# DeltaNet decay factors: from matrix products with triangles of ones to rows of a running-sum table, loaded per head

## The chip, the cores and the metric

One core of a Trainium2 chip runs the whole program. The metric is the device time of one execution in microseconds (us); lower is better. Five engines run their own instruction streams and wait for each other by semaphores: TensorE (PE in the rows; its weight loads are PEld), VectorE (DVE), ScalarE (ACT), GpSimd (POOL) and SyncE (SP). SP streams the weights; POOL and ACT issue the other DMA transfers, each on its own queue.

## The reference

A two-layer diffusion step: a neighbourhood-attention layer, then a gated DeltaNet layer, on 128 context tokens and 256 latent tokens. The change concerns the DeltaNet layer alone, for each of 32 value heads and two scan directions:

```python
gc = jnp.cumsum(g, axis=-1)
decay = jnp.exp(jnp.where(incl, gc[..., :, None] - gc[..., None, :], -jnp.inf))
kb = k * beta[..., None]
a_mat = (jnp.where(strict, jnp.einsum('bhnid,bhnjd->bhnij', kb, k) * decay, 0.0)
         + jnp.eye(DN_CHUNK, dtype=jnp.float32))
...
qk = jnp.einsum('bhnid,bhnjd->bhnij', q, k) * decay
...
    o_i = (jnp.einsum('bhcd,bhde->bhce', q_i * jnp.exp(g_i)[..., None], s)
           + jnp.einsum('bhij,bhje->bhie', qk_i, v_new))
```

`g` is a log decay per token and head, `gc` its running sum inside a chunk (of 128 tokens in the kernel: one context chunk, two latent ones), `decay` the matrix of exp(gc_i - gc_j), and exp(gc_i) scales the queries.

## The kernel before, in words

Weights arrive as 512 KB half tiles. ScalarE rounds each to a high part (`split_hi`, L403), VectorE subtracts to get the low part (`split_lo`, L412), and TensorE multiplies with three matmuls per 128x128 block (`multiply`, L445 to L447). Eight blocks make a half tile; in the plans one block, three matmuls of 384 columns, is one **part**.

The DeltaNet layer runs in phases, each engine through its own copy of the same plan. `ba` projects the gates and sums `g` with triangles of ones into tables for all heads. `dnP` projects the first key head (96 parts, no recurrence). `dn0` is a loop of 8 turns, `dn1` one of 7: each turn computes the recurrence of one key head (two value heads `v`, two directions `d`, so four units `u`) and between its steps projects the next key head. `dnE` is the last recurrence alone. Between `dn0` and `dn1` stand `ysplitA`, `fetchA`, `outA` (half of the output projection) and `keep1`. On entering a phase an engine waits at a barrier (`barrier`) until all other engines have done every counted step of the phases before. Inside the loops there are no barriers.

The order inside a turn is `DN_PLAN`: `merge` spreads the 96 parts among the steps of the chain by weights, a step of weight w standing after about 0.9 w further parts. The steps that matter here, in order: `norms` (sums of squares of q and k on TensorE, then logarithm and exponential on ScalarE, each with a table load), `decay` 0 to 2 and `broad` 1 and 2, `unit` (VectorE scales q and k), `gram` 0 to 2, `values`, then the triangular inversion from `left1` to `xf`, `recall`, `apply`, `state`, `out` (the last output products), `squares` and `out_norm`. After `out` come 4 parts, and 4 more in the next turn before `norms`.

A decay matrix of chunk c is made thus: POOL multiplies a triangle of ones by `g` of the next head into `g_mask` (`mask_steps`, L1487, which borrows the buffer `inv_c`), TensorE multiplies that by the other triangle into a bank of PSUM (L680; for `broad` by all ones, L686), ScalarE exponentiates the bank into `decay` (L988) or `q_dec` (L992). In `gram` VectorE reads the product of k with k and with q from PSUM (L1291), multiplies by `decay` and beta into `inv_c` (L1298), adds the directions (L1304) and the identity (L1307), and multiplies `decay` for the outputs (L1310); POOL then makes the first inversion buffer from `inv_c` (`right`, L1508), for which `left1` waits on TensorE (L784). GpSimd ends a turn with the gated outputs (`y`, L1532). TensorE's products go in turn to a ring of four banks; a product waits until the reader of the one four places before is done (`ring_free`).

```python
wait_steps(pool, turn, ("dve", "g_now"), *which)
lone()
for u in range(4):
    d, v = u // 2, u % 2
    i = nc.gpsimd.tensor_scalar(g_mask[c][:, u, :], K["le" if d == 0 else "ge"],
                                g_now[:, c, d, v:v + 1], 1.0, ALU.mult, ALU.mult)
```

Of the kernel before, what the change touches and what calls it, by code (L numbers as in the profile page):

```python
# [31 lines left out]
P = 128  # L32
# [113 lines left out]
def with_ada(halves):  # L146
    plan = []
    for k in halves:
# [13 lines left out]
_chain = [(5, ("norms",)), (2.5, ("decay", 0)), (2, ("decay", 1)), (1.5, ("broad", 1)), (0, ("unit",)), (2, ("decay", 2)),  # L162
          (1.5, ("broad", 2)), (1, ("gram", 0)), (2, ("gram", 1)), (2, ("gram", 2)), (1, ("values", 0)),
# [31 lines left out]
def dn_products():  # L195

    made = []
    for item in DN_CHAIN:
        what, arg = item[0], item[1] if len(item) > 1 else None
        if what == "decay":  # L200
            made.append((f"decay{arg}", "act"))
        elif what == "broad":
            made.append((f"broad{arg}", "act"))
        elif what == "norms":
# [24 lines left out]
def emit(nc, known, dram):  # L229
# [4 lines left out]
    with ExitStack() as ctx:  # L234
# [100 lines left out]
        for c in range(CHUNKS):  # L335
# [7 lines left out]
        decay = [region.take(f"decay{c}", [P, 4, P]) for c in range(CHUNKS)]  # L343
        q_dec = [None] + [region.take(f"q_dec{c}", [P, 4, P]) for c in (1, 2)]
# [4 lines left out]
        g_mask = [inv["c", c] for c in range(CHUNKS)]  # L349
# [6 lines left out]
                                 "halves_done", "evacuated", "small_in", "pairs_in", "x_in", "x_out", "bias_in", "k_out",  # L356
# [218 lines left out]
        def _(pe):  # L575
# [77 lines left out]
            def ba(pe, phase, turn):  # L653
# [10 lines left out]
                for n, masks in enumerate((("le", "ge"), ("gt", "lt"), ("ones", "ones"))):  # L664
# [5 lines left out]
                    done("pe", f"sums{n}", mm)  # L670

            def dn(pe, phase, turn):
                for item in DN_PLANS[phase]:
# [3 lines left out]
                    elif what == "decay":  # L677
                        wait_steps(pe, turn, ("pool", f"g_mask{arg}", True), ring_free(f"decay{arg}"))
                        for d, mask in enumerate(("gt", "lt")):
                            mm = nc.tensor.matmul(ring(f"decay{arg}")[:, 2 * d * P:(2 * d + 2) * P], K[mask],  # L680
                                                  g_mask[arg][:, 2 * d:2 * d + 2, :].rearrange("p v i -> p (v i)"),
                                                  start=True, stop=True)
                        done("pe", f"decay{arg}", mm)
                    elif what == "broad":
                        wait_steps(pe, turn, ring_free(f"broad{arg}"))
                        mm = nc.tensor.matmul(ring(f"broad{arg}")[:], K["ones"],  # L686
# [690 lines left out]
        def _(pool):  # L1377
# [257 lines left out]
```

## Time and profile before

| what | value |
|---|---|
| median of 3 runs | 2961.02 us (2958.56 to 2961.33) |
| the profiled execution's own time | 2958.55 us |
| its span | 2957.0 us |
| busy share of the span: PE, PEld, DVE, ACT, POOL | 89%, 85%, 64%, 40%, 24% |
| mean granted TensorE clock | 0.95 |
| share of the DMA queues: q1 (SP), q0 (POOL), q10 (ACT) | 24.5%, 8.6%, 2.6% |

A row of the timeline gives the start, the time that the group took, the engine, the line, the operation with the tensors it writes and reads, and in brackets how long the engine had been idle and what ended that. Matmuls are pipelined, so their own times overlap; what one costs is the distance from one start to the next. An fp32 matmul is recorded as two passes. Attention fills the first third of the span; `ba` begins about 1014 us into it, `dn0` at 1087, `outA` at 1877, `dn1` at 2026 and `dnE` at 2716.

### The profile page before, as it was taken

The numbers are of one execution on the slowest core, as the hardware profiler recorded it, in microseconds if no ns is written. First come the engines' busy times: TensorE is split into PE (matmuls) and PEld (weight loads), VectorE is DVE, ScalarE is ACT, GpSimd is POOL, SyncE is SP. The second block draws the span as 40 slices with busy tenths as digits, with TensorE's granted clock in tenths as the row PEclk, the third lists the DMA queues.
The fourth block names the chain that finished last, engine by engine and source line by source line (L and its number), as shares of the span: only waits on it lengthen the run. The fifth ranks groups of instructions, "written<-read, shape, count | busy, mean of one in ns | idle before, by whom it ended". The sixth has DMA issues, their size and how long they took to land. (4 is left out here: it accounts for less than half of the span.)

```text
span 2957.0 us, 51408 instructions
## 1 busy us (share of the span) xinstructions
PE 2625.2 (89%) x15405; PEld 2514.3 (85%) x15405; DVE 1906.8 (64%) x3821; ACT 1179.7 (40%) x2167; POOL 716.8 (24%) x1293
## 2 busy tenths in 40 slices
PE   2458999999989699999999999898999999998797
PEld 2458999999989598888988898897988899887697
DVE  2878888888853547666666667434676667665433
ACT  1024333333333533544444444323535453544322
POOL 2302222222211112332333233102234323332210
PEclk9999999999999799999999999998999999999699
DMA  8565666666643132212212121333222222211042
GB/s 236 190 218 205 234 228 232 222 233 233 228 167 125 67 133 72 75 64 71 75 68 71 65 76 66 125 127 117 73 75 68 66 73 71 75 64 57 25 150 92
DMA packets 115644, 363.06 MB, mean 123 GB/s; under 512 B 29072, under 2 KB 31248, under 8 KB 114640
## 3 DMA queue, kind: packets, MB, share of 16 engines
q1 hardware_dynamic: 69408, 252.74, 24.5%
q0 software_dynamic: 21280, 87.44, 8.6%
q10 hardware_dynamic: 24848, 21.82, 2.6%
q14 instruction: 86, 0.70, 0.1%
q8 instruction: 22, 0.36, 0.0%
HBM read 346.22 MB, written 15.73 MB: 122 GB/s over the span
## 5 line engine op out<-in xcount | busy, mean ns | idle before, releaser
L445 PE MATMUL bank<-h_hi,w_hi 128*128 128x384 f32 x2576 | 998.7, 388 | 47.8 <-DVE h_lo L1118 34.0
L447 PE MATMUL bank<-h_hi,w_lo 128*128 128x384 f32 x2576 | 884.9, 344 | 0.0
L446 PE MATMUL bank<-h_lo,w_hi 128*128 128x384 f32 x2576 | 882.4, 343 | 0.0
L412 DVE TENSOR_TENSOR w_lo<-raw,w_hi 128x512 fp32r<-128x512 f32 (+1 forms) x610 | 560.1, 925 | 306.4 <-ACT w_hi L403 254.1
L403 ACT ACTIVATE w_hi<-raw 128x512 fp32r<-128x512 f32 (+1 forms) x610 | 461.6, 792 | 369.1 <-PE bank L447 336.5
L445 PEld LDWEIGHTS bank<-h_hi,w_hi 128*128 128x128 f32 x2576 | 501.5, 195 | 71.3 <-issue 45.7
L446 PEld LDWEIGHTS bank<-h_lo,w_hi 128*128 128x128 f32 x2576 | 503.0, 195 | 13.5 <-issue 7.2
L447 PEld LDWEIGHTS bank<-h_hi,w_lo 128*128 128x128 f32 x2576 | 497.5, 193 | 0.0
L1083 DVE SCALAR_TENSOR_TENSOR ada_terms<-raw_ada,cond_rows 128x1024 f32<-128x1024 f32 x256 | 312.7, 1222 | 11.2 <-DMA raw_ada<-in_late 6.7
L445 PE MATMUL bank<-y_hi,w_hi 128*128 128x384 f32 x768 | 264.1, 344 | 33.2 <-DVE y_lo L1188 22.3
L1525 POOL CAST inv_x<-inv_x 128x128 fp32r<-128x128 f32 x576 | 211.6, 402 | 258.9 <-DVE inv_x L1355 258.3
L446 PE MATMUL bank<-y_lo,w_hi 128*128 128x384 f32 x768 | 262.9, 342 | 0.0
L447 PE MATMUL bank<-y_hi,w_lo 128*128 128x384 f32 x768 | 262.7, 342 | 0.0
L960 ACT ACTIVATE inv_turn<-bank 128x256 fp32r<-128x256 f32 x288 | 109.2, 386 | 344.4 <-PE bank L784 343.8
L784 PE MATMUL bank<-consts,inv_x 128*128 128x128 f32 x576 | 120.6, 297 | 92.5 <-POOL inv_x L1508 80.7
L1349 DVE TENSOR_TENSOR inv_cross<-bank,pairs 128x256 fp32r<-128x256 f32 x288 | 115.4, 422 | 134.3 <-PE bank L788 133.8
L784 PEld LDWEIGHTS bank<-consts,inv_x 128*128 128x128 f32 x576 | 79.1, 148 | 119.9 <-POOL inv_x L1508 99.3
L588 PE MATMUL bank<-cond,raw 128*128 128x2 f32 x384 | 84.8, 353 | 108.0 <-DMA raw<-in_stream 56.5
L445 PEld LDWEIGHTS bank<-y_hi,w_hi 128*128 128x128 f32 x768 | 148.5, 193 | 35.4 <-issue 23.5
L1423 POOL DMA_DIRECT2D raw_ada<-in_late x128 | 68.8, 538 | 450.0 <-DVE ada_terms L1083 359.1
L588 PEld LDWEIGHTS bank<-cond,raw 128*128 128x128 f32 x384 | 83.3, 331 | 109.5 <-DMA raw<-in_stream 57.9
L1083 DVE SCALAR_TENSOR_TENSOR ada_terms<-raw,cond_rows 128x1024 f32<-128x1024 f32 x80 | 125.4, 1567 | 71.1 <-ACT cond L857 49.7
(201 smaller groups left out, 3892.9 us busy)
## 6 DMA issues: line engine op xcount, KB each, us to landing
raw<-in_stream SPq DMA_DIRECT2D x482, 512.0 KB, 3.3
raw_ada<-in_late POOLq DMA_DIRECT2D x128, 512.0 KB, 3.6
x_kept<-y POOLq DMA_DIRECT2D x2, 3072.0 KB, 9.9
y<-x_kept POOLq DMA_DIRECT2D x2, 3072.0 KB, 11.1
bias<-in_rpb ACTq DMA_DIRECT2D x16, 256.0 KB, 6.5
S<-in_state ACTq DMA_DIRECT2D x16, 256.0 KB, 2.7
out_state_out<-s_out ACTq DMA_DIRECT2D x16, 256.0 KB, 2.0
y<-in_x ACTq DMA_DIRECT2D x1, 3072.0 KB, 20.8
```

The costliest lines, as they stand in the source:

```text
L403: nc.scalar.activation(w_hi[:, mk % SPLIT_SLOTS, w], raw[:, raw_n % RAW_SLOTS, w], ACT.Copy)\
L412: i = nc.vector.tensor_tensor(w_lo[:, mk % SPLIT_SLOTS, w], raw[:, raw_n % RAW_SLOTS, w], w_hi[:, mk % SPLIT_SLOTS, w].bitcast(F32), ALU.s ...
L445: nc.tensor.matmul(bank[:, 0:T], w_hi[:, slot, w], hi[:, kt, :], start=kt == 0, stop=False)
L446: nc.tensor.matmul(bank[:, 0:T], w_hi[:, slot, w], lo[:, kt, :], start=False, stop=False)
L447: last = nc.tensor.matmul(bank[:, 0:T], w_lo[:, slot, w], hi[:, kt, :], start=False, stop=kt == KT - 1)
L588: mm = nc.tensor.matmul(bank[:, 2 * tile:2 * tile + 2], weights[:, j * P:(j + 1) * P], cond[:, kt, :], start=kt == 0, stop=kt == KT - 1)
L784: mm = nc.tensor.transpose(bank[:, v * P:(v + 1) * P], now[:, v, :].bitcast(F32), K["ident"])
L960: done("act", name, nc.scalar.activation(dst, src, ACT.Copy))
L1083: i = nc.vector.scalar_tensor_tensor(ada_terms[:], weights, 1.0, cond_rows[:, g, half * HALF:(half + 1) * HALF], ALU.mult, ALU.mult, accum ...
L1349: done("dve", f"{name}_{c}", nc.vector.tensor_tensor(inv["cross", c][:], bank[:, 0:2 * P].rearrange("p (v i) -> p v i", v=2), pairs[:, n - ...
L1423: pool.dma_start(raw_ada[:, k % 2, :], dram["late"][bass.ds(8 * turn + k, 1)].rearrange("a p f -> p (a f)"))\
L1525: i = nc.gpsimd.tensor_copy(columns(after, turning, n, turning), columns(now, 0, n, turning).bitcast(F32))
```

## The change

`ba` now also turns the table of running sums (`banks[3]`, from L668) by a TensorE transpose, and POOL writes it to a DRAM tensor `rows`, one row of 128 sums per value head, chunk and direction. At the end of each turn (`squares`) POOL waits for `out` B, loads the rows of the next head, each spread over all 128 partitions, into `decays` (one transfer of 768 KB) and `q_decs` (two of 256 KB), waits for them, and subtracts each partition's own sum in place (`min` 0 keeps the unused triangle finite). ScalarE exponentiates both in place. The `decay` and `broad` steps leave TensorE's order and the ring; on ScalarE all five stand behind `norms`, and `gram` 0 now stands after 12 parts in place of 9.

```diff
-_chain = [(5, ("norms",)), (2.5, ("decay", 0)), (2, ("decay", 1)), (1.5, ("broad", 1)), (0, ("unit",)), (2, ("decay", 2)),
-          (1.5, ("broad", 2)), (1, ("gram", 0)), (2, ("gram", 1)), (2, ("gram", 2)), (1, ("values", 0)),
+_chain = [(5, ("norms",)), (0, ("decay", 0)), (0, ("unit",)), (0, ("decay", 1)), (0, ("decay", 2)), (0, ("broad", 1)),
+          (0, ("broad", 2)), (14, ("gram", 0)), (2, ("gram", 1)), (2, ("gram", 2)), (1, ("values", 0)),
...
-        decay = [region.take(f"decay{c}", [P, 4, P]) for c in range(CHUNKS)]
-        q_dec = [None] + [region.take(f"q_dec{c}", [P, 4, P]) for c in (1, 2)]
+        decays = region.take("decays", [P, 2, CHUNKS, 2, P])
+        q_decs = region.take("q_decs", [P, 2, CHUNKS - 1, 2, P])
...
@@ ba, on TensorE
+                wait_steps(pe, turn, ("act", "gc"))
+                for c in range(CHUNKS):
+                    mm = nc.tensor.transpose(banks[2][:, c * P:(c + 1) * P], bg[:, c, :], K["ident"])
+                done("pe", "rows", mm)
@@ dn, on TensorE
-                    elif what == "decay":
-                        wait_steps(pe, turn, ("pool", f"g_mask{arg}", True), ring_free(f"decay{arg}"))
-                        for d, mask in enumerate(("gt", "lt")):
-                            mm = nc.tensor.matmul(ring(f"decay{arg}")[:, 2 * d * P:(2 * d + 2) * P], K[mask],
-                                                  g_mask[arg][:, 2 * d:2 * d + 2, :].rearrange("p v i -> p (v i)"),
-                                                  start=True, stop=True)
-                        done("pe", f"decay{arg}", mm)
-                    elif what == "broad":
-                        wait_steps(pe, turn, ring_free(f"broad{arg}"))
-                        mm = nc.tensor.matmul(ring(f"broad{arg}")[:], K["ones"],
-                                              g_mask[arg][:].rearrange("p v i -> p (v i)"), start=True, stop=True)
-                        done("pe", f"broad{arg}", mm)
...
@@ ba, on ScalarE
+                done("act", "gc", nc.scalar.activation(bg[:, :, 64:P], banks[3][:, 0:CHUNKS * 2 * DN_V_HEADS]
+                                                       .rearrange("p (c h) -> p c h", c=CHUNKS), ACT.Copy))
@@ dn, on ScalarE
-                        wait_steps(act, turn, ("pe", f"decay{arg}"), ("pe", "outB", 1))
-                        done("act", f"decay{arg}", nc.scalar.activation(decay[arg][:].rearrange("p u i -> p (u i)"),
-                                                                        ring(f"decay{arg}")[:], ACT.Exp))
+                        wait_steps(act, turn, ("pool", f"exponent{arg}", True))
+                        done("act", f"decay{arg}", nc.scalar.activation(decay(arg), decay(arg), ACT.Exp))
...
+                        wait_steps(act, turn, ("pool", "exponent2", True))
+                        done("act", f"broad{arg}", nc.scalar.activation(q_dec(arg), q_dec(arg), ACT.Exp))
@@ ba, on VectorE
+                wait_steps(dve, turn, ("pe", "rows"))
+                done("dve", "rows", nc.vector.tensor_copy(bt[64:128, :], banks[2][64:128, 0:T]))
@@ keep1, on GpSimd
-                    mask_steps(pool, turn)
+                    exponents(pool, turn, GROUP, GROUP + 2)
@@ GpSimd
+            def ba(pool, phase, turn):
+                for d in range(2):
+                    wait_steps(pool, turn, ("dve", "rows"))
+                    rows = bt[64 + 32 * d:96 + 32 * d, :].rearrange("q (c i) -> q c i", c=CHUNKS)
+                    pool.dma_start(dram["rows"][:, :, d, :], rows).then_inc(s["rows_out"], 16)
+
+            def exponents(pool, turn, next_head, loads, *which):
+
+                wait_steps(pool, turn, ("dve", "g_now"), *which)
+                lone()
+                pool.wait_ge(s["rows_out"], 32)
+                rows = dram["rows"][bass.ds(2 * next_head, 2)].rearrange("v c d i -> (v c d i)").partition_broadcast(P)
+                pool.dma_start(decays[:].rearrange("p v c d i -> p (v c d i)"), rows).then_inc(s["rows_in"], 16)
+                for v in range(2):
+                    rows = dram["rows"][bass.ds(2 * next_head + v, 1), 1:CHUNKS].rearrange("v c d i -> (v c d i)").partition_broadcast(P)
+                    pool.dma_start(q_decs[:, v, :, :, :].rearrange("p c d i -> p (c d i)"), rows).then_inc(s["rows_in"], 16)
+                pool.wait_ge(s["rows_in"], 48 * loads)
+                lone()
                 for c in range(CHUNKS):
...
-                        i = nc.gpsimd.tensor_scalar(g_mask[c][:, u, :], K["le" if d == 0 else "ge"],
-                                                    g_now[:, c, d, v:v + 1], 1.0, ALU.mult, ALU.mult)
+                        i = nc.gpsimd.tensor_scalar(decay(c, u), decay(c, u), g_now[:, c, d, v:v + 1], 0.0,
+                                                    ALU.subtract, ALU.min)
...
@@ dn, on GpSimd, at squares
-                        mask_steps(pool, turn, ("pe", "applyB"))
+                        exponents(pool, turn, next_head, turn + {"dnP": 1, "dn0": 2, "dn1": GROUP + 3}[phase], ("pe", "outB"))
```

Two places in the order. First ScalarE in a turn of `dn0`, from the end of `norms` (`qk_rs`) to the splits of half tile 1 (`w_hi`). Before:

```order
L1002 ACTIVATE qk_rs_100<-qk_rs_100 128x386
L530 REGISTER_ALU
L988 ACTIVATE decay0_111<-bank4 128x512
L530 REGISTER_ALU
L988 ACTIVATE decay1_112<-bank5 128x512
L530 REGISTER_ALU
L992 ACTIVATE q_dec1_114<-bank2 128x512
L401 REGISTER_ALU
L403 ACTIVATE w_hi<-raw 128x512 x2
```

and with the change:

```order
L995 ACTIVATE qk_rs_100<-qk_rs_100 128x386
L531 ISA
L983 ACTIVATE decays_111<-decays_111 128x2x2x128
L531 REGISTER_ALU
L983 ACTIVATE decays_111<-decays_111 128x2x2x128
L531 REGISTER_ALU
L983 ACTIVATE decays_111<-decays_111 128x2x2x128
L986 ACTIVATE q_decs_112<-q_decs_112 128x2x2x128 x2
L402 REGISTER_ALU
L404 ACTIVATE w_hi<-raw 128x512 x2
```

Five exponentials stand ahead of the two splits where three stood.

Second VectorE in the same turn, from `unit` (`dn_qk`) to `gram` 0 and on to `gram` 1. Before:

```order
L1284 TENSOR_TENSOR dn_qk_106<-conv_117,qk_rs_100 128x256
L411 REGISTER_ALU
L412 TENSOR_TENSOR w_lo<-raw,w_hi 128x512
L530 REGISTER_ALU
L530 ISA
L1291 TENSOR_TENSOR gram_110<-bank5,consts 128x512
```

and with the change:

```order
L1279 TENSOR_TENSOR dn_qk_106<-conv_114,qk_rs_100 128x256
L412 REGISTER_ALU
L413 TENSOR_TENSOR w_lo<-raw,w_hi 128x512
L412 REGISTER_ALU
L413 TENSOR_TENSOR w_lo<-raw,w_hi 128x512
L412 REGISTER_ALU
L413 TENSOR_TENSOR w_lo<-raw,w_hi 128x512
L531 REGISTER_ALU
L531 ISA
L1286 TENSOR_TENSOR gram_110<-bank4,consts 128x512
```

Three splits stand between `unit` and `gram` 0 where one stood: the second of half tile 0, which came ahead of `unit`, and both of half tile 1, of which the second stood between `gram` 0 and `gram` 1.

## Rows read from the trace of the kernel before

**Rows 1.** Busy time by stretches of one turn: stretch, length, PE, PEld, DVE, ACT, POOL, clock, DMA.

```profile
1377.77:1393.60 15.83, 15.83 (x78) 13.49 (x77) 4.28 (x10) 15.40 (x24) 5.99 (x14) 1.00 0.26 84
1393.60:1409.10 15.50, 10.31 (x60) 9.10 (x58) 13.86 (x28) 4.58 (x13) 5.88 (x7) 0.84 0.10 35
1409.10:1417.00 7.90, 7.88 (x37) 7.86 (x38) 4.36 (x12) 1.70 (x4) 5.96 (x13) 0.67 0.21 66
1417.00:1474.70 57.70, 57.42 (x392) 55.55 (x391) 40.80 (x107) 24.04 (x59) 11.96 (x28) 1.00 0.23 78
```

**Rows 2.** Timeline of PE in a turn: `broad` 1, the second part after it, `decay` 2.

```profile
1292.10 1.02 PE L686 MATMUL bank<-inv_c,consts 128*128 128x512 f32 x2
...
1293.48 0.33 PE L445 MATMUL bank<-h_hi,w_hi 128*128 128x384 f32 x1
...
1294.00 1.02 PE L680 MATMUL bank<-inv_c,consts 128*128 128x256 f32 x4
```

**Rows 3.** Timeline of ACT in the turn of rows 1.

```profile
1391.00 1.06 ACT L988 ACTIVATE decay<-bank 128x512 f32<-128x512 f32 x2
...
1392.43 1.16 ACT L403 ACTIVATE w_hi<-raw 128x512 fp32r<-128x512 f32 x2
```

**Rows 4.** Timeline of DVE in the same turn, `unit` to `gram` 1.

```profile
1391.66 0.42 DVE L1284 TENSOR_TENSOR dn_qk<-conv,qk_rs 128x256 f32<-128x256 f32 x1
...
1394.49 0.69 DVE L1291 TENSOR_TENSOR gram<-bank,consts 128x512 f32<-128x512 f32 x1 [0.70 <-PE bank L701]
...
1398.33 1.25 DVE L412 TENSOR_TENSOR w_lo<-raw,w_hi 128x512 fp32r<-128x512 f32 x1
1399.49 0.68 DVE L1291 TENSOR_TENSOR gram<-bank,consts 128x512 f32<-128x512 f32 x1
```

**Rows 5.** Timeline of PE in the same turn: `left1` of the third chunk.

```profile
1409.12 0.69 PE L784 MATMUL bank<-consts,inv_x 128*128 128x128 f32 x2 [1.87 <-POOL inv_x L1508]
```

**Rows 6.** Timeline late in a turn: `apply` on ACT, then the output products on PE.

```profile
1850.70 1.16 ACT L1025 ACTIVATE v_newA<-bank,beta_now 128x128 f32<-128x128 f32 x4
...
1852.10 0.46 PE L766 MATMUL bank<-decay,v_newA 128*128 128x128 f32 x2
```

**Rows 7.** Timeline of DVE: `gram` 0 in the first turn of `dn0`, and in `dnE`.

```profile
1101.68 0.69 DVE L1291 TENSOR_TENSOR gram<-bank,consts 128x512 f32<-128x512 f32 x1 [2.62 <-PE bank L701]
...
2725.41 0.69 DVE L1291 TENSOR_TENSOR gram<-bank,consts 128x512 f32<-128x512 f32 x1 [2.39 <-PE bank L701]
```

**Rows 8.** Timeline of POOL at the end of a turn.

```profile
1384.08 1.98 POOL L1532 TENSOR_TENSOR y<-y,o_n 128x384 f32 x2 [2.29 <-DVE o_n L1339]
```

**Rows 9.** DMA issues: KB each, median us from issue to landing.

```profile
raw_ada<-in_late POOLq DMA_DIRECT2D x128, 512.0 KB, 3.6
x_kept<-y POOLq DMA_DIRECT2D x2, 3072.0 KB, 9.9
...
cond_rows<-in_cond_rows ACTq DMA_DIRECT2D x1, 2048.0 KB, 13.4
```

**Rows 10.** Busy time at the start, while the packets of `cond_rows` move; the last column is GB/s.

```profile
11.00:16.50 5.50, 0.00 (x0) 0.00 (x0) 0.00 (x0) 0.00 (x0) 0.00 (x0) 1.00 1.00 409
```

**Rows 11.** Timeline of PE on entering `dn0`, `outA`, `dn1` and `dnE`.

```profile
1086.88 0.68 PE L445 MATMUL bank<-h_hi,w_hi 128*128 128x384 f32 x1 [2.80 <-POOL inv_c L1487]
...
1876.70 0.66 PE L445 MATMUL bank<-y_hi,w_hi 128*128 128x384 f32 x1 [8.23 <-DVE y_lo L1188]
...
2026.20 0.68 PE L445 MATMUL bank<-h_hi,w_hi 128*128 128x384 f32 x1 [8.09 <-POOL inv_c L1487]
...
2716.37 2.91 PE L692 MATMUL bank<-qk_sq,consts 128*128 128x386 f32 x4 [4.84 <-POOL y L1532]
```

**Rows 12.** Timeline of POOL in `keep1`.

```profile
2019.43 0.54 POOL L1469 DMA_DIRECT2D x_kept<-y  x1 [136.21 <-DVE y L1205]
...
2021.58 4.18 POOL L1487 TENSOR_SCALAR inv_c<-consts,g_now 128x128 f32<-128x128 f32 x12
```

**Rows 13.** Timeline of PE at the end of `ba`, entering `dnP`.

```profile
1032.53 0.66 PE L445 MATMUL bank<-h_hi,w_hi 128*128 128x384 f32 x1 [1.03 <-ACT ada_terms L947]
```

More of the change, by code:

```diff
@@ L199, in dn_products @@
         what, arg = item[0], item[1] if len(item) > 1 else None
-        if what == "decay":
-            made.append((f"decay{arg}", "act"))
-        elif what == "broad":
-            made.append((f"broad{arg}", "act"))
-        elif what == "norms":
+        if what == "norms":
             made += [("ss0", "act"), ("ss1", "act")]
@@ L348, in emit @@
         pairs = region.take("pairs", [P, len(LEVELS), P])
-        g_mask = [inv["c", c] for c in range(CHUNKS)]
         overlay = Region(f32r_at - scratch_at)
@@ L1294, in dn @@
                             .rearrange("p (n d) i -> p n d i", n=2), ALU.mult))
-                        wait_steps(dve, turn, ("dve", f"gram{c}"), ("act", f"decay{c}"), ("pe", f"broad{max(c, 1)}"),
+                        wait_steps(dve, turn, ("dve", f"gram{c}"), ("act", f"decay{c}"),
                                    ("pe", "applyB", True))
                         for u in range(4):
-                            i = nc.vector.scalar_tensor_tensor(inv["c", c][:, u, :], decay[c][:, u, :],
+                            i = nc.vector.scalar_tensor_tensor(inv["c", c][:, u, :], decay(c, u),
                                                                beta_now[:, c, u // 2, u % 2:u % 2 + 1],
@@ L1308, in dn @@
                             inv["c", c][:], inv["c", c][:], K["ident"].unsqueeze(1).broadcast_to([P, 4, P]), ALU.add))
-                        both = decay[c][:].rearrange("p (d v) i -> p d v i", d=2)
+                        both = decay(c)
                         done("dve", f"masked{c}", nc.vector.tensor_tensor(
@@ L1478, in square_qk @@
                                                                       ALU.mult))
-            def mask_steps(pool, turn, *which):
+            def ba(pool, phase, turn):
[14 more added lines that the diff above has]
+                lone()
                 for c in range(CHUNKS):
-                    wait_steps(pool, turn, ("dve", "g_now"), *which)
-                    lone()
                     for u in range(4):
                         d, v = u // 2, u % 2
-                        i = nc.gpsimd.tensor_scalar(g_mask[c][:, u, :], K["le" if d == 0 else "ge"],
-                                                    g_now[:, c, d, v:v + 1], 1.0, ALU.mult, ALU.mult)
-                    done("pool", f"g_mask{c}", i)
+                        i = nc.gpsimd.tensor_scalar(decay(c, u), decay(c, u), g_now[:, c, d, v:v + 1], 0.0,
+                                                    ALU.subtract, ALU.min)
+                    done("pool", f"exponent{c}", i)
             def dn(pool, phase, turn):
-                head, _, row, _ = heads(phase, turn)
+                head, next_head, row, _ = heads(phase, turn)
                 for item in DN_PLANS[phase]:
@@ L1613, in declare @@
         dram |= {n: nc.dram_tensor(f"out_{n}", shape, F32, kind="ExternalOutput").ap() for n, shape in OUTS.items()}
+        dram["rows"] = nc.dram_tensor("rows", (DN_V_HEADS, CHUNKS, 2, P), F32).ap()
         dram["x_kept"] = nc.dram_tensor("x_kept", (P, KT, T), F32).ap()
```

22 lines of the change are left out of this document (11 added, 11 removed).

## The prediction

> **What bounds the kernel now.** I read the busy times of one turn of `dn0` by stretches first, then the timeline of each engine in it, then the starts of the phases. The page alone misleads: TensorE is busy for 89% of the span, so every product taken from it looks like time. By stretches a turn of 96.9 us shows three different limits [rows 1]. From the end of `out` B to `gram` 0 (15.8 us) TensorE is busy throughout, but so is ScalarE, with 15.40 of 15.83 us: square roots of the output norms, gates, a weight split, the q and k norms, with a table load between each, then the exponentials. From `gram` 0 to the last `left1` (15.5 us) TensorE is idle for 5.2 us and VectorE busy for 13.9; the last wait is for POOL's first buffer, made from what VectorE wrote [rows 5]. Only the remaining 65.6 us have TensorE alone as the limit. The products that leave lie in the first stretch. So the question is when VectorE can begin `gram` 0, since the chain gram, `inv_c`, POOL, `left1` follows from that at a fixed distance.
>
> **Off TensorE.** `broad` and the part behind it take 1.38 us, a part 0.52, so a product of 512 columns takes 0.86 us [rows 2]; `decay` has as many columns. Five a turn are 4.3 us, over 16 recurrences 68.8 us. `gram` 0 now stands behind three more parts (1.56 us), so TensorE would come to it 15.87 - 4.3 + 1.56 = 13.1 us behind `out` B, at 1390.9 on the clock of these rows. It needs `unit`, which ends at 1392.08 [rows 4], and that hangs on ScalarE's norms, which nothing shortens: TensorE waits 1.2 us there.
>
> **ScalarE and VectorE in a turn.** ScalarE starts its exponentials at 1391.00 as before. Two that read PSUM take 1.06 us, two weight splits of the same width, SBUF to SBUF, 1.16 [rows 3]; the new exponentials are SBUF to SBUF, so I take 0.525 each, 2.6 us for five, and the bounds 0.475 and 0.6 (2.4 and 3.0). The pair of splits of half tile 1 then runs from 1393.6 to 1394.8 in place of 1392.43 to 1393.59. VectorE must subtract both pieces ahead of `gram` 0 now; before, only the first. The second can start at 1394.8 and takes 0.6, so `gram` 0 starts at 1395.4 to 1395.5 in place of 1394.49 [rows 4]: 1.0 us later, where it waited 0.70 us for TensorE before. In return the subtraction between `gram` 0 and `gram` 1 is gone, 1399.49 - 1398.33 = 1.16 us [rows 4]. The two nearly cancel: `gram` 1, the POOL buffers and the last `left1`, at 1409.12 before [rows 5], come at the same time within 0.2 us. The 4.3 us of products are then waiting time of TensorE.
>
> What is won in a turn is what stands behind the last `left1`: two parts fewer (26 of 96 done there in place of 24), 1.04 us. Half of it is lost near the end: `state` A follows `apply` after two parts in place of three, and those three just covered ScalarE's `v_newA`, which ends at 1851.86 while TensorE's product starts at 1852.10 [rows 6]. I take 0.6 us a turn; the bounds are 0 and 1.2. There are 13 such turns: **-7.8 us** (0 to -15.6). In the first turn of each loop there is no ScalarE work left over from an `out` B, and VectorE waited 2.62 us for TensorE's `gram` 0 [rows 7]. There `gram` 0 comes about 2.4 us sooner (the splits bind then), 1.1 us goes with the subtraction, 0.6 as above: 4.1 us in each of two turns, **-8.2 us**.
>
> **The row loads.** POOL no longer makes its twelve tiles at once when VectorE's `g_now` is there: it waits for `out` B, issues 1280 KB in three transfers, waits for them, and only then works on its twelve tiles. The trace of before has no broadcast of this size on POOL's queue. By the rows of that queue, 512 KB land in 3.6 us and 3072 KB in 9.9 [rows 9], the straight line gives 5.5 us for 1280 KB. The low bound is 3.6 us. The high one is 13.4 us, for the 2048 KB of `cond_rows`, a broadcast like this one, but issued behind seven smaller ones; while its packets move the queues carry 409 GB/s [rows 10], so spreading one row over 128 partitions is not slow by itself, and I take 5.5. In a turn this is hidden: the twelve tiles (4.2 us [rows 12], one operation per 128x128 tile as before) are done about 10 us behind `out` B, and ScalarE wants the last at 14.3, when two exponentials are through. The cover is 4 us; it is gone when a load takes more than 9.6. POOL's gated outputs `y`, queued behind, start 10.1 us behind `out` B in place of 6.3 [rows 8]; in a loop nobody waits for them by then. DMA engines have room: POOL's queue is 8.6% of the span and a turn moves 71 GB/s or so [rows 1].
>
> **At the barriers nothing hides it.** Four times an engine waits at a phase's start for these POOL steps [rows 11]. `dn0`: TensorE waited 2.80 us for the twelve tiles; they now start a load later, +5.5. `outA`: y_lo follows `y`, which ends 3.9 to 4.0 us later, +4.0. `dnE`: TensorE waited 4.84 us for `y`, +4.0; this recurrence gets back 1.4, for there VectorE waits 2.39 us for TensorE's `gram` 0 [rows 7], of which the product itself needs about 1. `dn1`: in `keep1` POOL first issues `x_kept`, 3072 KB, at 2019.43, and started the tiles at 2021.58 [rows 12]. The row loads go out on the same queue behind it. If they move only when it has landed (9.9 us), they end at 2019.43 + 9.9 + 3.1 (1280 KB by the slope of rows 9) = 2032.5, +10.9; if they move beside it, +5.5. I take 10.9, since one queue carries both. The Trainium skill, "DMA: Bandwidth & Descriptors", section "Queues, rings and completion order", says that each engine consumes the descriptors of a ring in their order; by that rule it is 10.9 too, without it the sum would be 5.4 lower. `ba` gains a copy, three transposes and a copy in a chain ahead of `dnP`; each handoff to TensorE there is about 1 us [rows 13]: +2.0 (1 to 3). Together 2.0 + 5.5 + 4.0 + 2.6 + 10.9 = **+25.0 us**.
>
> **Sum.** 25.0 - 7.8 - 8.2 = +9.0. The profiled execution took 2958.55 us, so 2967.6; its own time lies 2.5 us under the median of 2961.02. By the bounds of the load in the barriers (3.6 us: -7.6 over four), of the queue (-5.4) and of the turns (-7.8 to +7.8) which are independent (the root of the sum of their squares is 12), the forecast's own range is 2955 to 2980. A measurement of this kernel can tell about 0.2% from no change, 5.9 us.
>
> **Rivals.**
> 1. *VectorE's `gram` 0 is freed (faster).* If ScalarE gets the splits done before `unit`, so that VectorE starts `gram` 0 as soon as TensorE's product allows, at about 1393.0 in place of 1395.5, the chain starts 2.5 us earlier in 13 turns: -32.5, 2935 us. It decides when `gram` 0 starts within 15.3 us of `out` B. For it: TensorE is there early, and the products were what VectorE waited for [rows 4]. Against it: ScalarE's order and its 15.40 of 15.83 us [rows 1]. Chance 0.28.
> 2. *The loads are slow (slower).* With the 13.4 us of rows 9, ScalarE waits 3.8 us in each of 13 turns (+49) and the four barriers grow by 7.9 each (+32): 3049 us. It decides at 9.6 us. Against it: 409 GB/s during a broadcast [rows 10]. The Trainium skill (same page, section "Latency and other measured facts") has copies at row pitches of 4 MiB fall to 103 GB/s and infers that streams in lock-step meet on the same memory channels; 128 copies of one row would be the extreme of that, and by that figure I estimate 12.7 us for the bytes alone. The one broadcast in this trace does not agree. Chance 0.08.
> 3. *TensorE's clock (slower).* The stretch behind the last `left1` runs at 0.67 of the clock after 5.2 us of idling [rows 1], some 5.2 of its 7.9 us at half speed, which costs 2.6 us. TensorE now idles for about 10 us between `unit` and the last `left1`. If the half-speed stretch behind it doubles in 13 turns, +34: 3001 us. For it: the idling comes in more and longer pieces. Against it: the work up to the last `left1` hides in the waits at either speed, and behind it TensorE is as busy as before. Chance 0.10.
>
> **How the numbers follow.** The forecast has 0.50: 0.22 of it lies within 5.9 us of no change, 0.28 above; 0.04 is left for the products' whole 68.8 us. Faster by over 0.2%: 0.28 + 0.04 = 0.32. Within: 0.22, and 0.02 for rival 3 with a third of its price or less, 0.24. Slower: 0.28 + 0.08 + 0.10 less that 0.02 = 0.44. The range reaches down past rival 1, by what it would give with 15% more, and up nearly to rival 3: 2930 to 2998. What lies outside is rival 2, the edges of 1 and 3, and the rest, 0.2.
>
> **What would show it.** In a turn: ScalarE's exponentials without a wait for POOL; VectorE's `gram` 0 about 17.7 us behind `out` B, released by ScalarE's split, not by TensorE; no subtraction between `gram` 0 and 1; the last `left1` about 31.3 us behind `out` B as before; TensorE idle for 10 us in the first two stretches; a turn of 96.3 us. The waits at the four phase starts: about 8.3, 12, 19 and 8.8 us. Wrong would be the forecast if turns are shorter than 95 us (rival 1), if ScalarE waits for POOL in the turns (rival 2), or if the stretch at half clock behind the last `left1` exceeds 8 us (rival 3).

## The result and the profile after

The changed kernel takes 3022.64 us (median of 4 runs, 3019.46 to 3025.48), the kernel before 2959.79 us in the same comparison: ratio 1.0211, 95% interval [1.0199, 1.0223], 63 us slower. The prediction said 2967.6 us, range 2930 to 2998: the sign was right, the size was far off, and the time lies outside the range. The profiled executions compared below have spans of 2957.0 us (before) and 3020.5 us (after), 63.5 us apart.

Where the 63.5 us are is found by measuring the distances between two marks that every recurrence has, TensorE's first `norms` product and ScalarE's first `o_sq` (the squares behind `out` B). The turns after the first of each loop, seven in `dn0` and six in `dn1`, are called steady here. For the seven of `dn0` the marks are these rows of ScalarE's timeline, first and last, of the kernel before:

```profile
1183.12 0.87 ACT L1036 ACTIVATE o_sq<-bank 128x384 f32<-128x384 f32 x2 [0.79 <-PE bank L769]
...
1865.09 0.87 ACT L1036 ACTIVATE o_sq<-bank 128x384 f32<-128x384 f32 x2 [0.79 <-PE bank L769]
```

and after:

```profile
1193.21 0.88 ACT L1029 ACTIVATE o_sq<-bank 128x384 f32<-128x384 f32 x2 [1.21 <-PE bank L762]
...
1890.25 0.88 ACT L1029 ACTIVATE o_sq<-bank 128x384 f32<-128x384 f32 x2 [1.21 <-PE bank L762]
```

Seven turns took 681.97 us and now take 697.04. Counted in this way over the whole program (us, after less before; the last column is experiment 1, below):

| stretch | predicted | after | e1 |
|---|---|---|---|
| start to the first `norms` of `dn0` | +7.5 | +13.6 | +11.7 |
| first turns of `dn0` and `dn1` | -8.2 | -9.0 | -7.5 |
| 13 steady turns | -7.8 | +29.2 | -8.0 |
| last `o_sq` of `dn0` to the first `norms` of `dn1` | +14.9 | +22.5 | +14.2 |
| end of `dn1` to the `o_sq` of `dnE` | +2.6 | +9.0 | +7.1 |
| the rest | 0 | -1.8 | -1.9 |
| sum | +9.0 | +63.5 | +15.7 |

Two kinds of stretch are wrong: the steady turns, which should have won a little and lose 2.25 us each, and the phase starts. Both have the same engine in them. The timeline of POOL at the end of a turn of `dn0` after the change:

```profile
1392.63 0.61 POOL L1487 DMA_DIRECT2D decays<-rows  x1 [2.37 <-PE bank L762]
1393.25 1.12 POOL L1490 DMA_DIRECT2D q_decs<-rows  x2
1399.23 9.34 POOL L1496 TENSOR_SCALAR decays<-decays,g_now 128x128 f32<-128x128 f32 x12 [4.86 <-DMA q_decs<-rows]
1408.55 1.99 POOL L1541 TENSOR_TENSOR y<-y,o_n 128x384 f32 x2
```

From the first issue to the last landing is 6.6 us, a little more than the 5.5 that was forecast. But the twelve tile operations, which took 4.2 us in the kernel before [rows 12], take 9.34 us, and `y`, queued behind them, starts 17.0 us behind `out` B in place of 6.3 [rows 8] (the end of `out` B is counted, as in rows 1, from 0.28 us ahead of the start of `o_sq`: 1391.60 here). ScalarE's timeline in the same turn shows who waits:

```profile
1404.84 1.14 ACT L983 ACTIVATE decays<-decays 128x512 f32<-128x512 f32 x2
1408.61 0.63 ACT L983 ACTIVATE decays<-decays 128x512 f32<-128x512 f32 x1 [2.63 <-POOL decays L1496]
1409.14 1.14 ACT L986 ACTIVATE q_decs<-q_decs 128x512 f32<-128x512 f32 x2
1410.19 1.14 ACT L404 ACTIVATE w_hi<-raw 128x512 fp32r<-128x512 f32 x2
```

and VectorE's timeline what stands behind that:

```profile
1405.93 0.68 DVE L413 TENSOR_TENSOR w_lo<-raw,w_hi 128x512 fp32r<-128x512 f32 x1
1410.84 1.29 DVE L413 TENSOR_TENSOR w_lo<-raw,w_hi 128x512 fp32r<-128x512 f32 x2 [4.23 <-ACT w_hi L404]
1412.05 0.68 DVE L1286 TENSOR_TENSOR gram<-bank,consts 128x512 f32<-128x512 f32 x1
```

ScalarE waits 2.63 us for the third chunk's tiles; the weight splits queued behind its exponentials come that much later; VectorE idles 4.23 us for them and starts `gram` 0 at 1412.05, 20.5 us behind `out` B. It was 16.7 before [rows 4]. The busy times by stretches of this turn (`out` B to the first `gram` product, to the last `left1`, to the next `out` B; columns as in rows 1):

```profile
1391.60:1406.06 14.46, 13.25 (x71) 11.86 (x69) 3.31 (x9) 13.95 (x20) 8.53 (x13) 1.00 0.43 147
1406.06:1425.84 19.78, 10.07 (x56) 8.58 (x56) 14.60 (x29) 6.98 (x17) 10.02 (x13) 0.83 0.15 53
1425.84:1490.70 64.86, 64.19 (x430) 62.41 (x431) 45.94 (x120) 25.09 (x61) 16.90 (x40) 0.97 0.23 77
```

The last `left1` comes 34.2 us behind `out` B in place of 31.3, and TensorE idles 1.2 and 9.7 us ahead of it. The stretch behind it is 64.9 us, at a mean clock of 0.97 where it was 0.96, so the half clock costs no more there than it did before. The 65.6 us of rows 1, with which it would be compared, end 0.9 us early: `o_sq` of the next turn, in ScalarE's timeline of the kernel before, shows the end of `out` B 0.28 us ahead of it, at 1475.63 and not at 1474.70.

```profile
1475.91 0.87 ACT L1036 ACTIVATE o_sq<-bank 128x384 f32<-128x384 f32 x2 [0.78 <-PE bank L769]
```

That turn took 97.9 us; the steady turns before are 96.8 and 97.9 by turns, 97.4 on the mean. Over all thirteen the stretch behind the last `left1` went from 66.0 to 65.2 us on the mean, about as much as was forecast to be won there (0.6).

The phase starts, by TensorE's timeline (`dn0`, `outA`, `dn1`, `dnE`, to be held against rows 11):

```profile
1100.11 0.68 PE L446 MATMUL bank<-h_hi,w_hi 128*128 128x384 f32 x1 [15.74 <-POOL decays L1496]
...
1911.89 0.66 PE L446 MATMUL bank<-y_hi,w_hi 128*128 128x384 f32 x1 [18.27 <-DVE y_lo L1181]
...
2073.88 0.68 PE L446 MATMUL bank<-h_hi,w_hi 128*128 128x384 f32 x1 [23.71 <-POOL decays L1496]
...
2782.06 2.91 PE L685 MATMUL bank<-qk_sq,consts 128*128 128x386 f32 x4 [14.23 <-POOL y L1541]
```

The four waits were forecast at 8.3, 12, 19 and 8.8 us; they are 4.7 to 7.4 us longer than that.

### The profile page after: what moved, and what is told of

It reads as the page before. It is cut to its first block and busy times, and to the rows that moved or that the text cites. A ratio compares the mean times of both kernels' runs of the same rounds, so it can differ in the third digit from the quotient of the medians.

```text
span 3020.5 us, 50882 instructions
## 1 busy us (share of the span) xinstructions
PE 2568.7 (85%) x15152; PEld 2470.1 (82%) x15152; DVE 1907.2 (63%) x3822; ACT 1177.8 (39%) x2168; POOL 803.6 (27%) x1346
## 5 line engine op out<-in xcount | busy, mean ns | idle before, releaser
L446 PE MATMUL bank<-h_hi,w_hi 128*128 128x384 f32 x2576 | 979.7, 380 | 77.2 <-POOL decays L1496 39.5
L404 ACT ACTIVATE w_hi<-raw 128x512 fp32r<-128x512 f32 (+1 forms) x610 | 469.7, 789 | 530.2 <-PE bank L448 467.7
L1076 DVE SCALAR_TENSOR_TENSOR ada_terms<-raw_ada,cond_rows 128x1024 f32<-128x1024 f32 x256 | 312.8, 1222 | 11.7 <-DMA raw_ada<-in_late 7.0
L1534 POOL CAST inv_x<-inv_x 128x128 fp32r<-128x128 f32 x576 | 195.0, 376 | 263.7 <-DVE inv_x L1350 263.5
L1496 POOL TENSOR_SCALAR decays<-decays,g_now 128x128 f32<-128x128 f32 x204 | 153.7, 767 | 91.3 <-DMA q_decs<-rows 91.3
```

The lines of the kernel that those rows point to most:

```text
L404: nc.scalar.activation(w_hi[:, mk % SPLIT_SLOTS, w], raw[:, raw_n % RAW_SLOTS, w], ACT.Copy)\
L446: nc.tensor.matmul(bank[:, 0:T], w_hi[:, slot, w], hi[:, kt, :], start=kt == 0, stop=False)
L1076: i = nc.vector.scalar_tensor_tensor(ada_terms[:], weights, 1.0, cond_rows[:, g, half * HALF:(half + 1) * HALF], ALU.mult, ALU.mult, accum ...
L1496: i = nc.gpsimd.tensor_scalar(decay(c, u), decay(c, u), g_now[:, c, d, v:v + 1], 0.0, ALU.subtract, ALU.min)
L1534: i = nc.gpsimd.tensor_copy(columns(after, turning, n, turning), columns(now, 0, n, turning).bitcast(F32))
```

## The experiments

Three things were open: whether POOL's operation itself is slow or something around it; whether ScalarE's wait is what lengthens the turn; and whether the idea, with that mended, gains what leaves TensorE.

**1. Multiply in place of subtract and minimum, on POOL.**

```diff
-                        i = nc.gpsimd.tensor_scalar(decay(c, u), decay(c, u), g_now[:, c, d, v:v + 1], 0.0,
-                                                    ALU.subtract, ALU.min)
+                        i = nc.gpsimd.tensor_scalar(decay(c, u), decay(c, u), g_now[:, c, d, v:v + 1], 0.0,
+                                                    ALU.mult, ALU.mult)
```

> POOL's twelve tile operations use multiply and multiply in place of subtract and minimum; same tiles, still in place (the exponents are other numbers). Theory: the pair of operations sets the price. A tile takes 0.35 us in place of 0.77, twelve 4.2 us in place of 8.3 to 9.3; ScalarE's wait of 2.63 us for POOL in a turn goes, turns come down from 99.6 to about 97.0 us (13 x 2.6 = 34 us) and the four phase starts are 4.1 us earlier each (16 us): 2972 us. Rival A: working in place, or data just loaded, is what is slow: tiles stay at 0.77 us, 3022 us. Rival B: TensorE's half-speed stretches lengthen the turn and not ScalarE's wait: tiles are quick, the phase starts give 16 us, the turns stay at 99 us: 3006 us.

Measured: 2976.38 us, ratio to the kernel before, run beside it, 1.0052 [1.0035, 1.0068]. The tile operations by their line, first of the changed kernel:

```profile
L1496 POOL TENSOR_SCALAR decays<-decays,g_now x204: 704/709/1252, 1091.3 to 2779.2; 128x128 f32<-128x128 f32 x102
```

then of this one (shortest, median and longest in ns):

```profile
L1496 POOL TENSOR_SCALAR decays<-decays,g_now x204: 361/362/902, 1093.6 to 2730.3; 128x128 f32<-128x128 f32 x102
```

Same tiles, same buffer in place, same loads: half the time. ScalarE's wait for POOL is gone from its list of waits, and a steady turn takes 96.8 us. The theory holds; rival A (working in place) and rival B (the clock) fall: the turns came down with the price of one operation alone. In the last column of the table above the turns and the stretch from `dn0` to `dn1` stand within 0.7 us of the forecast; the starts of `dn0` and `dnE` stay 4.2 and 4.5 us above it. The four waits at the phase starts, by TensorE's timeline, are 3.0, 2.1, 0.5 and 2.0 us above the forecast ones even with quick tiles:

```profile
1098.21 0.68 PE L446 MATMUL bank<-h_hi,w_hi 128*128 128x384 f32 x1 [11.30 <-POOL decays L1496]
...
1886.85 0.66 PE L446 MATMUL bank<-y_hi,w_hi 128*128 128x384 f32 x1 [14.13 <-DVE y_lo L1181]
...
2044.69 0.68 PE L446 MATMUL bank<-h_hi,w_hi 128*128 128x384 f32 x1 [19.52 <-POOL decays L1496]
...
2732.79 2.91 PE L685 MATMUL bank<-qk_sq,consts 128*128 128x386 f32 x4 [10.78 <-POOL y L1541]
```

**2. Which operation is slow.** Chunk by chunk other operations, in two kernels.

```diff
-                        i = nc.gpsimd.tensor_scalar(decay(c, u), decay(c, u), g_now[:, c, d, v:v + 1], 0.0,
-                                                    ALU.subtract, ALU.min)
+                        if c == 0:
+                            i = nc.gpsimd.tensor_scalar(decay(c, u), decay(c, u), g_now[:, c, d, v:v + 1], 0.0,
+                                                        ALU.subtract, ALU.mult)
+                        elif c == 1:
+                            i = nc.gpsimd.tensor_scalar(decay(c, u), decay(c, u), g_now[:, c, d, v:v + 1], 0.0,
+                                                        ALU.mult, ALU.min)
+                        else:
+                            i = nc.gpsimd.tensor_scalar(decay(c, u), decay(c, u), g_now[:, c, d, v:v + 1], None,
+                                                        ALU.subtract)
...
+                        i = nc.gpsimd.tensor_scalar(decay(c), decay(c), 0.0, None, ALU.min)
```

> One look at prices on POOL: chunk 0 subtract and multiply, chunk 1 multiply and minimum, chunk 2 subtract alone per tile and then one minimum over 512 columns (the exponents of chunks 0 and 1 are other numbers). Theory 1: minimum is the slow one: chunk 0 0.35 us a tile, chunk 1 0.77, subtract alone under 0.35. Theory 2: subtract is the slow one: chunk 0 0.77, chunk 1 0.35. Theory 3: any pair but multiply and multiply is slow: 0.77 in chunks 0 and 1, single operations 0.35 or less.

The lines of the three chunks, and the minimum over 512 columns:

```profile
L1497 POOL TENSOR_SCALAR decays<-decays,g_now x68: 707/713/1227, 1092.1 to 2806.0; 128x128 f32<-128x128 f32 x68
L1500 POOL TENSOR_SCALAR decays<-decays,g_now x68: 704/715/1167, 1094.9 to 2808.8; 128x128 f32<-128x128 f32 x68
L1503 POOL TENSOR_SCALAR decays<-decays,g_now x68: 594/602/1148, 1097.7 to 2811.2; 128x128 f32<-128x128 f32 x68
L1509 POOL TENSOR_SCALAR decays<-decays x17: 1490/1492/1496, 1100.2 to 2812.0; 128x512 f32<-128x512 f32 x17
```

Both pairs, one with subtract and one with minimum, take 0.71 us; subtract alone still takes 0.60. It is not the numbers that are slow: chunk 0 here, from the same rows, ends in zeros as the quick pair of experiment 1 does. Theories 1 and 2 fall; theory 3 holds for these pairs but not for the single operation. The second kernel tried multiplications and additions (`ALU.add, ALU.mult`; `ALU.mult, ALU.add`; one `ALU.mult` by a constant, in the same three places).

> One look at prices on POOL, other operations in place of subtract and minimum: chunk 0 add and multiply, chunk 1 multiply and add, chunk 2 one multiplication by a constant (the exponents are other numbers). If multiplication is what is quick: chunk 2 at most 0.36 us a tile, chunks 0 and 1 0.7. If only the pair multiply and multiply is quick: chunk 2 takes 0.6 us as the single subtraction did, and chunks 0 and 1 0.7. If multiply and add are both quick and subtract and minimum slow: all at 0.36.

```profile
L1497 POOL TENSOR_SCALAR decays<-decays,g_now x68: 356/362/368, 1093.1 to 2726.7; 128x128 f32<-128x128 f32 x68
L1500 POOL TENSOR_SCALAR decays<-decays,g_now x68: 362/362/795, 1094.5 to 2728.2; 128x128 f32<-128x128 f32 x68
L1503 POOL TENSOR_SCALAR decays<-decays x68: 517/520/952, 1095.9 to 2730.0; 128x128 f32<-128x128 f32 x68
```

None of the three forecasts fits whole: pairs of multiply and add are quick in either order, as the third says, but one multiplication by a constant takes longer (0.52 us) than a pair. So on POOL the price depends on which operations are asked for, and fewer is not quicker. Why this is so was not tried. The turns follow the price: a steady turn takes 101.6 us in the first of these two kernels and 96.7 in the second.

**3. The row loads ahead of `x_kept`.** In `keep1`, same calls in another order:

```diff
+                if phase == "keep1":
+                    exponents_load(pool, turn, GROUP)
                 pool.dma_start(dram["x_kept"], x[:]).then_inc(s["x_out"], 16)
                 if phase == "keep1":
                     square_qk(pool, turn)
-                    exponents(pool, turn, GROUP, GROUP + 2)
+                    exponents(pool, turn, GROUP + 2)
...
```

`exponents` is split for this: `exponents_load` issues the loads, and what is left of `exponents` waits for them and makes the tiles.

> In keep1 POOL issues the row loads ahead of the 3 MB store of x_kept in place of behind it. Theory (the loads wait in the queue behind the store): POOL's wait there, 9.83 us, becomes 4.9 as at the other phase starts, dn1 starts 5 us earlier, 3017.6 us. Rival (store and loads share the DMA engines, the order of issue is nothing): the wait stays within 1 us of 9.8 less the shift, the time within 1 us of 3022.

Measured: 3020.69 us, ratio 1.0186 [1.0169, 1.0203], which alone could not be told from 1.0211. The trace can: POOL waits 3.44 us for the rows in place of 9.83, and `dn1` starts after 17.66 us of TensorE's waiting in place of 23.71, 6.0 us less. (The whole stretch from `dn0` to `dn1` is 4.2 us shorter, and other stretches of this execution are longer by as much.)

```profile
2071.47 0.68 PE L446 MATMUL bank<-h_hi,w_hi 128*128 128x384 f32 x1 [17.66 <-POOL decays L1500]
```

The loads had waited behind the store, as the prediction took it.

**4. `y` ahead of the tiles.**

```diff
...
                             done("pool", f"y{v}", nc.gpsimd.tensor_tensor(
                                 y_row(row + v), y_row(row + v), o_n[:, v, :], ALU.mult))
+                        if phase != "dnE":
+                            exponents(pool, turn, turn + {"dn0": 2, "dn1": GROUP + 3}[phase])
```

> POOL issues the row loads where it did, but makes the gated outputs y ahead of its twelve tile operations. Theory (a turn hangs on the tiles through ScalarE's wait, the starts of outA and dnE hang on y): y ends 8.3 us earlier, outA starts 8.3 us earlier and dnE some 5; the tiles start 0.9 us later, ScalarE's wait grows from 2.63 to 3.5 us, 13 turns lose 0.9 each, 12 us: 3021 us in all. Rival (ScalarE's wait for POOL does not set the turn): the turns stay at 99.6 us and 13 us are won: 3009 us.

Measured: 3030.27 us, ratio 1.0226 [1.0208, 1.0243]. Both forecasts missed. The turns lost 0.6 us (100.2 in place of 99.6), less than the 0.9 expected, but the phase starts gave back little: `outA` waits 16.54 us in place of 18.27, and `dnE`, in TensorE's timeline,

```profile
2790.51 2.91 PE L685 MATMUL bank<-qk_sq,consts 128*128 128x386 f32 x4 [13.16 <-POOL decays L1499]
```

now waits for the tiles. At `outA` ScalarE's first reading of `y` shows the same: `y` is done at 1904.51, and `y_hi` starts when the tiles behind it are done, at 1912.82:

```profile
1902.57 1.94 POOL L1546 TENSOR_TENSOR y<-y,o_n 128x384 f32 x2 [3.53 <-DVE o_n L1334]
1904.51 8.31 POOL L1499 TENSOR_SCALAR decays<-decays,g_now 128x128 f32<-128x128 f32 x12
1912.93 2.86 ACT L908 ACTIVATE y_hi<-y 128x1536 fp32r<-128x1536 f32 x2 [9.10 <-POOL decays L1499]
```

The barrier waits for every counted step of POOL, and the tiles are counted, so it makes no difference which of the two comes last. The reason given for +4.0 at `outA` and `dnE` ("y_lo follows `y`") was too narrow.

**5. The tiles on VectorE.** POOL issues the loads; VectorE does the same twelve operations behind `o_n`.

```diff
...
+            def exponents(dve, turn, loads):
+                wait_steps(dve, turn, ("dve", "g_now"))
+                dve.wait_ge(s["rows_in"], 48 * loads)
+                for c in range(CHUNKS):
+                    for u in range(4):
+                        d, v = u // 2, u % 2
+                        i = nc.vector.tensor_scalar(decay(c, u), decay(c, u), g_now[:, c, d, v:v + 1], 0.0,
+                                                    ALU.subtract, ALU.min)
+                    done("dve", f"exponent{c}", i)
...
                                 o_n[:, v, :], banks[6 + v][:, 0:T], dn_norm_w[:, 0:1], o_rs[:, v, :], ALU.mult, ALU.mult))
+                        if next_head is not None:
+                            exponents(dve, turn, turn + {"dn0": 2, "dn1": GROUP + 3}[phase])
```

> The twelve subtract-and-minimum operations go from POOL to VectorE, behind the output norms o_n; POOL only issues the row loads, where it did. Theory (POOL's price for these operations is what makes the change slow): VectorE's tile operations take 0.25 to 0.28 us by its other 128x128 operations, 3.0 to 3.4 us for twelve, in a stretch where it waits; ScalarE no longer waits for them, turns 96.0 to 96.8 us in place of 99.6 (some -40 us), the starts of dn0 and dn1 are 5 us earlier, of outA and dnE 6 to 8 us (-24 in all): about 2959 us, the time of before within 6 us. Rival A: the pair is as slow on VectorE (0.7 us), twelve take 9 us and stand ahead of unit: turns over 101 us, 3040 us or more. Rival B: what makes the turns longer is TensorE's half-speed stretch: turns stay at 99 us, about 2997 us.

Measured: 2949.55 us, ratio 0.9970 [0.9957, 0.9983]; the time forecast was 2959 and a turn of 96.0 to 96.8 us. VectorE's timeline in a turn, with the end of `out` B at 1369.86:

```profile
1378.19 2.44 DVE L1232 TENSOR_SCALAR decays<-decays,g_now 128x128 f32<-128x128 f32 x12 [1.80 <-DMA q_decs<-rows]
...
1386.34 1.29 DVE L413 TENSOR_TENSOR w_lo<-raw,w_hi 128x512 fp32r<-128x512 f32 x2 [1.57 <-ACT w_hi L404]
1387.55 0.68 DVE L1303 TENSOR_TENSOR gram<-bank,consts 128x512 f32<-128x512 f32 x1
```

Twelve take 2.44 us, in a stretch where VectorE only waited. The steady turn is 96.7 us, as forecast. The waits at the starts of `dn0`, `outA`, `dn1` and `dnE` are 1.03, 10.60, 17.77 and 7.18 us; they gave back more than the forecast's 24 us, which is why the time is 10 us under it. `gram` 0 waits for ScalarE's splits, 17.7 us behind `out` B, as the prediction had it.

**6. Two splits out of the chain.** On the base of 5, VectorE's splits of half tile 1 go behind the third `gram`:

```diff
-                    if what == "part" and item[2] in LO_AT:
+                    if what == "part" and item[2] in LO_AT and (arg != 1 or head is None):
                         split_lo(dve, phase, turn, arg + LOOKAHEAD, LO_AT.index(item[2]))
...
                             both, both, gram[:, 1, :, :].unsqueeze(2).broadcast_to([P, 2, 2, P]), ALU.mult))
+                        if c == CHUNKS - 1 and phase != "dnE":
+                            for piece in range(2):
+                                split_lo(dve, phase, turn, 1 + LOOKAHEAD, piece)
```

> As e5, and the two weight splits of half tile 1 on VectorE come behind the third gram step in place of ahead of the first. Theory (rival 1 of the prediction: gram 0 is what the turn hangs on, and it waits for splits rather than for TensorE): gram 0 starts about 15.5 us behind out B in place of 17, the chain to the last left1 comes 1.2 to 1.8 us earlier, 13 turns give 16 to 23 us against e5: about 2940 us. Rival (the splits only move, and TensorE or the splits themselves come late behind them): within 5 us of e5.

Measured: 2924.42 us, ratio 0.9882 [0.9865, 0.9898]; a turn of 94.8 us, and 25 us less than experiment 5, a little more than forecast. And as a control the same edit in the kernel before, with its products:

> The kernel before, with its products on TensorE, and only the two weight splits of half tile 1 on VectorE put behind the third gram step. Theory (the products of this change were in the way of gram 0 as much as the splits): gram 0 hangs on TensorE's product, which stands behind the decay products and ends 0.2 us after unit's chain allows, so gram 0 stays where it is, gram 1 comes 1.2 us earlier, 13 turns give 10 to 16 us: about 2947 us, 20 us or more behind e6. Rival (the order of the splits is the whole gain of e6 and e8 and the change of the decays gives nothing): 20 to 25 us won as e6 won them against e5, about 2936 us or less.

Measured: 2947.35 us, ratio 0.9963 [0.9950, 0.9975], as its theory had it; a turn of 96.7 us. VectorE's `gram` 0 in the two, experiment 6 (`o_sq` of that turn starts at 1371.26):

```profile
1386.30 0.69 DVE L1303 TENSOR_TENSOR gram<-bank,consts 128x512 f32<-128x512 f32 x1 [0.41 <-PE bank L694]
```

and the control (`o_sq` at 1375.75):

```profile
1392.19 0.69 DVE L1291 TENSOR_TENSOR gram<-bank,consts 128x512 f32<-128x512 f32 x1 [2.40 <-PE bank L701]
```

With the products in the way, VectorE is ready 2.4 us sooner and waits for TensorE: `gram` 0 stays 16.4 us behind `o_sq`. Without them it is 15.0. Taking the products away (with the splits left in place: 0.30% won in 5) and taking the splits away (alone: 0.37%) give 1.18% together, nearly twice the sum: each gain was in part hidden behind the other wait. By the steady turn, which leaves the phase starts out: 97.4 us before, 96.7 with either edit, 94.8 with both.

**7. The rows early, and all together.** On the base of 5, loads ahead of `x_kept` in `keep1`, and loads and tiles inside `dnP`.

> As e5, and the row loads stand early: in dnP ahead of its first part (VectorE's tiles in its middle), in keep1 ahead of the store of x_kept. Theory (at the phase starts nothing hides load and tiles): the wait at dn0 goes down to 2 us or less (8 to 10 us won), that at dn1 by 5 to 6 us: 13 to 16 us under e5, 2945 us. Rival (another step is as late at these starts): under 6 us won.

Measured: 2946.63 us, ratio 0.9953 [0.9937, 0.9970]. At `dn1` the wait fell from 17.77 to 11.98 us, as expected; at `dn0` there was nothing to win, since it waited 1.03 us in experiment 5 already: POOL no longer waits for `g_now` there, and its loads went out 16 us ahead of VectorE's tiles. So less than 6 us was won, as the rival had it, and that the time stands near the forecast 2945 is luck: experiment 5, the base, lay 10 us under its own forecast.

> e6 and e7 together. If both theories hold and the gains add, 30 to 38 us under e5, about 2925 us, 1.2% under the kernel before; if gram 0 earlier only moves the wait, about the time of e7.

Measured: 2918.15 us (2915.87 to 2920.26), ratio 0.9858 [0.9842, 0.9875]: 42.5 us under the kernel before and 31 under experiment 5, within the forecast, the fastest version here. TensorE's five products leave, VectorE takes the tiles, and the two splits leave the chain.

## Why the prediction was wrong

**The step that failed** is in the paragraph on the row loads: "the twelve tiles (4.2 us [rows 12], one operation per 128x128 tile as before) are done about 10 us behind `out` B". The tiles are as many and as wide as before, but the operations are not: multiply and multiply became subtract and minimum. A tile costs 0.71 us at a phase start and 0.78 in a turn in place of 0.35, the twelve 8.3 and 9.3 us, and they are done 17.0 us behind `out` B, past the 14.3 at which ScalarE wants the last. With the old pair of operations (experiment 1) they are done at about 12.8, and ScalarE does not wait. The cover of 4 us was named, and the load that would use it up; the tiles' price, taken from a row of another operation, had no bounds. The Trainium skill ("GPSIMD Engine Reference", section "3.1 Elementwise — side-by-side cycle accounting") says that up to two arithmetic operations per element the loop is limited by reading and writing, which would make one price for all these pairs; the trace does not agree (0.36 and 0.71 us). The price of this step alone is the difference between the changed kernel and experiment 1: 63.5 - 15.7 = 47.8 us of span, of which 37 lie in the 13 steady turns and most of the rest at the phase starts.

**Right, once that price is taken out** (experiment 1): the 13 turns, -7.8 forecast and -8.0 measured, and the first turns, -8.2 and -7.5. The turn of 96.3 us was reckoned from one of 96.9, read 0.9 us short; 0.6 less than the mean of 97.4 is 96.8, as measured. `gram` 0 was expected 17.7 us behind `out` B and stood there in experiments 1 and 5, in 5 released by ScalarE's split. So the main claim holds: TensorE's 68.8 us of products are for the most part waiting time as long as VectorE's splits stand ahead of `gram` 0. The stretch from `dn0` to `dn1` came out near the forecast, +14.2 for +14.9, partly by luck: its two waits grew by 5.9 and 11.4 us, 17.3 together, and `outA` itself became 3.1 us shorter, which was not forecast; in the kernel before TensorE waited 3.81 us for a weight split inside it, in experiment 1 only 1.98.

**Smaller misses.** Experiment 1 lies 6.7 us above the sum of +9.0, mostly at the starts of `dn0` and `dnE`. The loads took longer than the 5.5 us forecast: from the first issue to the start of the tiles 6.2 to 7.4 us in the turns of the changed kernel, of which POOL's three issues are 1.7, and 8.4 at the start of `dn0`, where nothing hides it. At `outA` and `dnE` the barrier counts the tiles and not `y` alone (experiment 4). The 1.4 us that `dnE` was to get back did not come in experiment 1: from its `norms` to its `o_sq` it took 71.9 us, before 70.7.

**`ba`** cost what was forecast, 2.0 us. `dnP` starts at 1031.90 us, no later than before [rows 13], but `ba` itself began earlier in that execution. TensorE's first product of the gates before:

```profile
1022.06 0.90 PE L660 MATMUL bank<-consts,bgT 128*128 128x128 f32 x3 [7.46 <-DVE bgT L1220]
```

and after, with its first of `dnP`:

```profile
1019.54 0.90 PE L661 MATMUL bank<-consts,bgT 128*128 128x128 f32 x3 [7.47 <-DVE bgT L1213]
...
1031.90 0.66 PE L446 MATMUL bank<-h_hi,w_hi 128*128 128x384 f32 x1 [1.37 <-issue]
```

From the one to the other it is 10.5 us before and 12.4 after, 1.9 more. The first row of the table, +13.6, is 2.5 us too small by this chance.

**The rivals.** The changed kernel has the shape of rival 2 (ScalarE waits for POOL, all four starts grow), but not its cause: by the page a load of 768 KB lands in 4.8 us and one of 256 KB in 5.0, with the rows spread over 128 partitions. Rival 1 was a real gain behind the wrong gate: it came only when the splits were moved (experiment 6), not from the change itself. Rival 3 did not happen: behind the last `left1` the mean clock is 0.97, and was 0.96. The order in which one queue's transfers go was read rightly (experiment 3): the loads waited for the store ahead of them.

## What to carry to other kernels

When an instruction keeps its shape but gets other operations, its old duration is no price: look for a row with the same operations on the same engine, and where there is none, bound it and move the bound through every place that waits for it. Work taken from the engine that looks busy is worth little (0.6 of 4.3 us a turn in experiment 1) until the step that feeds the next wait can start earlier; here two edits gave 0.30% and 0.37% alone and 1.18% together, because each hid the gain of the other. And a barrier that counts steps makes a phase wait for every counted step of an engine, also for those that nobody reads there.

## What the runs showed of the hardware

On POOL a 128x128 fp32 operation took 0.36 us for multiply-multiply, add-multiply and multiply-add, 0.60 for one subtraction and 0.71 for the three pairs tried with subtract or minimum, all with one scalar per partition, and 0.52 for one multiplication by a constant (experiments 1 and 2). VectorE did subtract and minimum at 0.20 us a tile (2.44 us for twelve, experiment 5).

In experiment 1 a short VectorE operation took six times its usual time beside POOL's `y`, which ran from 1398.78 to 1400.75:

```profile
1399.11 1.78 DVE L1278 TENSOR_TENSOR dn_qk<-conv,qk_rs 128x128 f32<-128x128 f32 x1 [0.46 <-ACT qk_rs L995]
1400.82 0.41 DVE L1279 TENSOR_TENSOR dn_qk<-conv,qk_rs 128x256 f32<-128x256 f32 x1
1401.15 0.28 DVE L1278 TENSOR_TENSOR dn_qk<-conv,qk_rs 128x128 f32<-128x128 f32 x1
```

The same operation takes 0.28 us two rows on, when POOL is done. It is no accident of one turn: in experiment 1 all eighteen `dn_qk` operations that start while `y` runs end 0.15 or 0.16 us (the 128x128 ones) or 0.28 us (the 128x256 ones) behind the end of one of the two operations of `y`, and the 128x128 ones take between 0.29 and 2.05 us, by how early they start. So in these rows VectorE's operation ends only when POOL's is through. No run was made to try this by itself.
